# Wide matmuls in q, k and the down projections, a final norm taken in behind the transposes, and other orders in attention

## What is computed

```python
for i in range(DEPTH):                       # DEPTH = 4
    kind = i % N_MIXERS                      # 0 mLSTM, 1 windowed, 2 neighbourhood attention
    mod = (silu(cond) @ ada_w[i] + ada_b[i]).reshape(6, D_MODEL)
    h = _rmsnorm(x, norm_w[i, 0]) * (1.0 + mod[1]) + mod[0]
    x = x + mod[2] * mixer(h)
    h = _rmsnorm(x, norm_w[i, 1]) * (1.0 + mod[4]) + mod[3]
    x = x + mod[5] * _conv_ffn(h, ffn_w_up[i], ffn_conv_w[i], ffn_conv_b[i], ffn_w_down[i])
y = _rmsnorm(x, final_norm_w)
```

## Time and profile before

| | |
|---|---|
| median of 3 executions | 1898.17 us (1898.11 to 1900.09) |
| profiled execution | 1898.71 us, span of its instructions 1896.9 us |
| TensorE busy | 1835.8 us, 97% of the span |
| VectorE busy | 1312.5 us, 69% |
| ScalarE busy | 980.9 us, 52% |
| GpSimd busy | 177.7 us, 9% |
| mean granted TensorE clock | 0.990 of full |
| memory traffic | 418 MB, mean 220 GB/s |

### The profile page before, as it was taken

One profiled execution on the slowest core, in us unless ns is written; L12 is line 12 of the kernel. 1 busy time (PEld: TensorE's weight loads), 2 busy tenths in 40 slices (PEclk: granted clock), 3 DMA queues, 4 the chain that ended last, 5 costly groups with the idle time before them and its releaser, 6 DMA issues.

```text
span 1896.9 us, 29734 instructions
## 1 busy us (share of the span) xinstructions
PE 1835.8 (97%) x12336; PEld 1577.7 (83%) x12336; DVE 1312.5 (69%) x1871; ACT 980.9 (52%) x1453; POOL 177.7 (9%) x154
## 2 busy tenths in 40 slices
PE   5999999999999999999999999999999999999998
PEld 2999877797889867889976778898999777988898
DVE  2854677667896566898555688956654776669974
ACT  1754344545674454676344466745643445447752
POOL 2100121001000112000111210002100220020001
PEclk9999999999999999999999999999999999999999
DMA  8565656866554657655574766556555647645451
GB/s 350 198 225 189 203 181 246 315 232 270 236 198 179 267 221 293 241 226 184 194 296 151 291 268 259 181 195 240 226 181 170 222 174 283 256 164 191 179 194 50
DMA packets 72535, 418.26 MB, mean 220 GB/s; under 512 B 12176, under 2 KB 18696, under 8 KB 24144
## 3 DMA queue, kind: packets, MB, share of 16 engines
q1 hardware_dynamic: 53856, 392.19, 55.3%
q10 hardware_dynamic: 18544, 24.17, 4.0%
HBM read 405.35 MB, written 10.95 MB: 219 GB/s over the span
## 4 chain that ended last, share of the span: by engine, by line
PE 88%; DVE 5%; DMA 2%; ACT 2%; issue 2%; POOL 1%; ACTq 0%; POOLq 0%; SPq 0%; DVEq 0%
PE ps L560 17%; PE ps L578 9%; PE ps L562 9%; PE ps L612 6%; PE ps L614 6%; PE ps L613 6%; PE ps L543 6%; PE ps L545 6%; PE ps L544 6%; PE ps L594 4%; PE ps L625 3%; DMA raw<-in_stream 2%; DVE spl_lo L466 1%; PE ps L831 1%; PE ps L816 1%
## 5 line engine op out<-in xcount | busy, mean ns | idle before, releaser
L466 DVE TENSOR_TENSOR spl_lo<-raw,spl_hi 128x1024 fp32r<-128x1024 f32 x556 | 687.7, 1259 | 275.3 <-ACT spl_hi L455 274.3
L455 ACT ACTIVATE spl_hi<-raw 128x1024 fp32r<-128x1024 f32 x556 | 573.9, 1052 | 327.0 <-PE ps L614 161.5
L560 PE MATMUL ps<-H,spl_hi 128*128 128x512 f32 x1408 | 497.5, 399 | 3.4 <-DVE H L1669 3.4
L562 PE MATMUL ps<-H,spl_lo 128*128 128x256 f32 x1408 | 393.9, 280 | 0.0
L560 PEld LDWEIGHTS ps<-H,spl_hi 128*128 128x128 f32 x1408 | 265.0, 188 | 78.2 <-issue 14.6
L562 PEld LDWEIGHTS ps<-H,spl_lo 128*128 128x128 f32 x1408 | 266.1, 189 | 0.0
L612 PE MATMUL ps<-G_hi,spl_hi 128*128 128x256 f32 x704 | 199.2, 283 | 0.0
L613 PE MATMUL ps<-G_lo,spl_hi 128*128 128x256 f32 x704 | 199.2, 283 | 0.0
L614 PE MATMUL ps<-G_hi,spl_lo 128*128 128x256 f32 x704 | 199.2, 283 | 0.0
L543 PE MATMUL ps<-H,spl_hi 128*128 128x256 f32 x512 | 148.2, 289 | 6.8 <-DVE H L1669 5.2
L544 PE MATMUL ps<-H,spl_hi 128*128 128x256 f32 x512 | 146.0, 285 | 0.0
(11 more groups left out here) (241 smaller groups left out, 3226.6 us busy)
## 6 DMA issues: line engine op xcount, KB each, us to landing
raw<-in_stream SPq DMA_DIRECT2D x374, 1024.0 KB, 4.9
out_new_C<-c_stage ACTq DMA_DIRECT2D x16, 512.0 KB, 3.7
ada_b<-in_ada_b ACTq DMA_DIRECT2D x4, 768.0 KB, 9.2
E<-rows_out ACTq DMA_DIRECT2D x8, 256.0 KB, 4.3
Em<-rows_out ACTq DMA_DIRECT2D x8, 256.0 KB, 4.7
x<-in_x ACTq DMA_DIRECT2D x1, 1024.0 KB, 12.1
wide<-rows_out ACTq DMA_DIRECT2D x8, 128.0 KB, 5.2
cache<-in_na_cache ACTq DMA_DIRECT2D x1, 1024.0 KB, 9.0
```

The source lines that it names most:

```text
L455: act.activation(spl_hi[m % SPL][:, :], raw[r % RAW][:, h * HALF:(h + 1) * HALF], ACT.Copy).then_inc(S["hi_done"], 1)
L466: dve.tensor_tensor(spl_lo[m % SPL][:, :], raw[r % RAW][:, h * HALF:(h + 1) * HALF], spl_hi[m % SPL][:, :].bitcast(F32), ALU.subtract).the ...
L560: pe.matmul(banks[:, b * 512:(b + 1) * 512], w_hi, H[:, kk * 512:(kk + 1) * 512], start=kk == 0, stop=False, skip_group_check=True)
L562: mm = pe.matmul(banks[:, b * 512:b * 512 + TOK], w_lo, H[:, kk * 512:kk * 512 + TOK], start=False, stop=kk == KD - 1, skip_group_check=True)
```

## The change

- q and k are computed in wide form (`queries_keys`). `A_hi` and `A_lo` become the two halves of one tensor A, `B_hi` and `B_lo` of B, at the places that they had; a chunk's high and low columns stay 16 KB apart, and a wide matmul reads them as two runs of 256 columns (`A_both`, `B_both`). ACT copies the high half of each bank to Q or K and DVE adds the low half (`with_low`). The banks are ACC[0:4], two for each group of two tiles.
- The mLSTM and FFN down projections are wide for pairs 0 to 2 and narrow for pair 3 (`project_wide`). Pair p uses banks 2p and 2p+1; pair 3 uses ACC[0] once pair 0 has been added. The gated activations lie chunk by chunk, as H does. `residual` adds a wide pair in two passes of four instructions.
- The final norm: DVE's scaled x is transposed without the inverse root, three of four groups of transposes before the sum of squares; the root is a per-row factor when ACT and DVE evacuate the rows. The broadcast matmul and the four products fall away. Three of the four output transfers move from ACT's queue to SP's.
- One adaLN tile is placed between the halves of v; the first head of layer 0 and the last head of layer 3 have one less.
- ACT's row broadcasts of the second head of each mLSTM layer are issued behind two splits of v's weights, not in front.
- Layer 1: ACT's transposed queries(1) stands in front of exps(3). Layer 2: DVE's reciprocals(1) stands in front of the split.
- The state of the last head in layer 3 uses banks ACC[2:4], and TensorE waits for pair 2's addition before the normalisers of two norms.

```diff
+V_FILL = 1
-HEAD_FILL = {0: [3, 3, 3, 2], 3: [2, 2, 2, 2]}
+HEAD_FILL = {0: [2, 3, 3, 2], 3: [2, 2, 2, 1]}
+WIDE = [r for r in range(2 * DEPTH) if r % 2 or MIXER[r // 2] == "mlstm"]
...
-            order += [("ml_v", i, c, t) for c in range(2) for t in range(8)]
+            order += [("ml_v", i, 0, t) for t in range(8)]
+            fill(V_FILL)
+            order += [("ml_v", i, 1, t) for t in range(8)]
...
+    A = sb("A", 2 * KI * TOK, F32R, rA)
+    A_hi, A_lo = A[:, 0:KI * TOK], A[:, KI * TOK:2 * KI * TOK]
+    A_both = A[:, :].rearrange("p (e k t) -> p k e t", e=2, t=TOK)
...
+            sp.wait_ge(S["yrow_a"], 2)
+            sp.dma_start(io["y_prompt"][0, :, 0:512], yrow[:, 0:512]).then_inc(S["y_landed"], 16)
+            sp.wait_ge(S["yrow_d"], 2)
+            sp.dma_start(io["y_prompt"][0, :, 512:D], yrow[:, 512:D]).then_inc(S["y_landed"], 16)
+            sp.wait_ge(S["yrow_d"], 4)
+            sp.dma_start(io["y_sample"][0, :, 512:D], yrow[:, D + 512:2 * D]).then_inc(S["y_landed"], 16)
...
+            def queries_keys(n, k0, banks):
+                for h in range(2):
+                    m = 2 * n + h
+                    pe.wait_ge(S["lo_done"], m + 1)
+                    for k in range(4):
+                        kk = k0 + 4 * h + k
+                        for b in range(2):
+                            c = slice(k * 256 + b * P, k * 256 + b * P + P)
+                            w_hi, w_lo = spl_hi[m % SPL][:, c], spl_lo[m % SPL][:, c]
+                            pe.matmul(v3(banks[b][:, :], TOK), w_hi, B_both[:, kk], start=kk == 0, stop=False,
+                                      skip_group_check=True)
+                            mm = pe.matmul(banks[b][:, 0:TOK], w_lo, B_both[:, kk, 0], start=False, stop=kk == KI - 1,
+                                           skip_group_check=True)
+                    mm.then_inc(S["half_used"], 1)
...
+            def project_wide(n0, t, nk, r, rows, chunk, ready):
...
+                        if pair < 3:
+                            bank = ps[2 * pair + o]
+                            pe.matmul(v3(bank[:, :], TOK) if nk == KI else bank[:, :], w_hi, rows(k), start=k == 0, stop=False, skip_group_check=True)
+                            mm = pe.matmul(bank[:, 0:TOK], w_lo, chunk(k)[0], start=False, stop=k == nk - 1,
+                                           skip_group_check=True)
+                            continue
+                        if k == 0 and o == 0:
+                            pe.wait_ge(S["x_done"], 5 * r + 1)
...
                 if q in (1, 2 * DEPTH - 1):
+                    pe.wait_ge(S["x_done"], 5 * (q - 1) + 3)
                     normalisers()
...
-                    if t % 2 == 0:
-                        pe.wait_ge(S["qk_evac"], 8 * j + t // 2 + 1)
-                    weights_stationary(n0 + t, both(B_hi, B_lo), 8 * (t % 2), UP[(t // 2) % 2], t % 2 == 0, t % 2 == 1)
+                    if t % 2 == 0 and 4 * j + t // 2 >= 2:
+                        pe.wait_ge(S["qk_sum"], 2 * (8 * j + t // 2) - 2)
+                    queries_keys(n0 + t, 8 * (t % 2), ACC[t // 2 % 2 * 2:t // 2 % 2 * 2 + 2])
...
-                pe.wait_ge(S["qk_evac"], 2 + 8 * (j + 1))
+                pe.wait_ge(S["qk_sum"], 16 * (j + 1))
...
-                    project(n0, t, 2 * NJ, both(G_hi, G_lo), ready)
+                    project_wide(n0, t, 2 * NJ, 2 * i + 1, lambda k: G[:, k * 512:(k + 1) * 512], both_of(G), ready)
...
-            norm(2 * DEPTH)
             for g in range(4):
-                pe.wait_ge(S["hm_done"], 4 * 2 * DEPTH + g + 1)
+                if g == 3:
+                    square_sums(2 * DEPTH)
+                if g < 2:
+                    pe.wait_ge(S["x_done"], 5 * (2 * DEPTH - 1) + 3)
+                pe.wait_ge(S["xa_done"], g + 1)
                 for s in range(NS):
                     for c in range(2):
                         k = 2 * g + c
-                        mm = pe.transpose(ACC[g][:, s * TOK + c * P:s * TOK + (c + 1) * P],
-                                          yT[:, k * TOK + s * T:k * TOK + (s + 1) * T], ident)
+                        mm = pe.transpose(ROWS[g][:, s * TOK + c * P:s * TOK + (c + 1) * P],
+                                          xa[:, k * TOK + s * T:k * TOK + (s + 1) * T], ident)
...
-                    copy(K[:, g * 512:(g + 1) * 512], UP[g % 2][:, :], "qk_evac")
+                    for b in range(2):
+                        copy(K[:, g * 512 + b * TOK:g * 512 + (b + 1) * TOK], ACC[g % 2 * 2 + b][:, 0:TOK], "qk_evac")
...
-                for h in range(2):
-                    state_rows(j, h)
+                state_rows(j, 0)
...
+                        if half == 0 and t == 1:
+                            state_rows(j, 1)
...
+                    queries(1, ACC[0])
                     exps(3)
-                    queries(1, ACC[0])
...
+            act.wait_ge(S["rstd_done"], 2 * DEPTH + 1)
+            for s in range(NS):
+                for g in range(2):
+                    act.wait_ge(S["yt_mm"], g + 1)
+                    act.activation(y_columns(s, g), ROWS[g][:, s * TOK:(s + 1) * TOK], ACT.Identity,
+                                   scale=rstd[:, s:s + 1]).then_inc(S["yrow_a"], 1)
...
+                wide = WIDE.index(r) if r in WIDE else None
+                if wide is not None and pair < 3:
+                    for e in range(2):
+                        for c in range(4):
+                            k, s = divmod(4 * pair + c, NS)
+                            o = slice(k * TOK + s * T, k * TOK + (s + 1) * T)
+                            ins = dve.scalar_tensor_tensor(x[:, o], ps[k][:, e * TOK + s * T:e * TOK + (s + 1) * T],
+                                                           coef_g[r % 2][:, NS * k + s:NS * k + s + 1], x[:, o],
+                                                           ALU.mult, ALU.add)
+                        ins.then_inc(S[("x_half", "x_done")[e]], 1)
+                        if e == 0:
+                            dve.wait_ge(S["x_half"], 3 * wide + pair + 1)
...
+                def with_low(dst, g, done, scale):
+                    for b in range(2):
+                        o = slice(g * 512 + b * TOK, g * 512 + (b + 1) * TOK)
+                        dve.wait_ge(S["qk_evac"], 16 * j + 2 * done + b + 1)
+                        dve.scalar_tensor_tensor(dst[:, o], ACC[g % 2 * 2 + b][:, TOK:2 * TOK], scale, dst[:, o], ALU.mult,
+                                                 ALU.add).then_inc(S["qk_sum"], 1)
...
                     maxima(1)
+                    reciprocals(1)
                     split("qkv", i, 1, 1, 0)
-                    reciprocals(1)
```

More of the change, by code:

```diff
@@ L596, in half_rows @@
                                                stop=t == h == k == 1 and a is a_lo, skip_group_check=True)
+                    mm.then_inc(S["half_used"], 1)
+            def project_wide(n0, t, nk, r, rows, chunk, ready):
+                for h in range(2):
+                    m = 2 * (n0 + t) + h
+                    pe.wait_ge(S["lo_done"], m + 1)
+                    ready(2 * t + h)
+                    for c in range(8):
+                        pair, k, o = unit(16 * t + 8 * h + c, nk)
+                        w_hi, w_lo = (w[m % SPL][:, c * P:(c + 1) * P] for w in (spl_hi, spl_lo))
+                        if pair < 3:
[6 more added lines that the diff above has]
+                            pe.wait_ge(S["x_done"], 5 * r + 1)
+                        x_hi, x_lo = chunk(k)
+                        out = ACC[0][:, o * TOK:(o + 1) * TOK]
+                        st, en = k == 0 and o == 0, k == nk - 1 and o == 1
+                        pe.matmul(out, w_hi, x_hi, start=st, stop=False, skip_group_check=True)
+                        pe.matmul(out, w_hi, x_lo, start=False, stop=False, skip_group_check=True)
+                        mm = pe.matmul(out, w_lo, x_hi, start=False, stop=en, skip_group_check=True)
                     mm.then_inc(S["half_used"], 1)
@@ L687, in norm @@
                     if late:
-                        state(1, MH - 1, range(2, 3), ACC[0:2])
+                        state(1, MH - 1, range(2, 3))
                     fill(between)
@@ L691, in norm @@
                     if late:
-                        state(1, MH - 1, range(3, 4), ACC[0:2])
+                        state(1, MH - 1, range(3, 4))
                 fill(after)
@@ L818, in values, with state @@
                     mm.then_inc(S["half_used"], 1)
-            def state(j, h, parts=range(4), banks=ACC[2:4]):
+            def state(j, h, parts=range(4)):
                 q = 4 * j + h
@@ L1153, in norm @@
                 if late:
-                    state(1, MH - 1, range(3), ACC[0:2])
+                    state(1, MH - 1, range(3))
                 for g in range(4):
@@ L1630, in mod_columns, with scaled @@
                                                   nw.unsqueeze(2).to_broadcast([P, KD, 2]), ALU.add, ALU.mult))
-            def scaled(pair):
```

(8 more changed lines are left out.)

85 lines of the change are left out of this document (44 added, 41 removed).

## The result

The changed kernel takes 1871.74 us (median, 1869.12 to 1873.76), the kernel before, timed beside it, 1898.11 (1892.71 to 1900.09): a ratio of 0.9876, 95% interval 0.986 to 0.9893, so 26.4 us less. Timed twice more, beside experiments, it took 1873.65 against 1893.26 (ratio 0.9895, 0.988 to 0.9911) and 1873.11 against 1893.17 (0.9893, 0.9879 to 0.9908), 20 us less. The forecast, 1876 and 22 us less, lies between.

A forecast was written before the change was run, and what follows sets the result against it. TensorE, busy 1835.8 of 1896.9 us, was taken as the bound. Terms 12.3 + 1.8 + 5.0 + 0.3 + 4.5 - 1.2 = 22.7 us, off the median 1898.17, gave 1875.5, said as 1876; range 1867 to 1887.

The forecast's parts named there:

- Wide units: q, k, mixer and FFN down projections: 1232 units made wide save 0.010 us each, 12.3 us; 3.4 to 16.3.
- the middle: Pace of a wide unit taken as 0.350 us, between 0.3536 and 0.3468 seen in the FFN's up projection.
- End of k: TensorE waits for the last group's copies and dependent DVE sums: cost 0.6 us per layer, 1.2 us; 0.4 to 2.
- The tile in v: An adaLN tile of 0.9 us fits in TensorE's 1.4 us wait mid-v: gain 1.8 us over two layers; 1 to 2.
- DVE at pair ends: Wide pairs' eight DVE adds instead of four delay the next weight split 1.2 us, covered by about 1.4 us: no cost.
- 18 pair ends: Ends of wide down-projection pairs; without the cover of about 1.4 us, each would cost what is missing.
- Layer 2: Attention, reciprocal of unit 1 before DVE's split: 4.3 us of idle plus 1 us at half clock, taken as 5.0; 2 to 6.5.
- Late next: Layer 2 attention: after the reciprocal moves, the copy of the query rows, still behind the split, is what comes late.
- Layer 1: Attention, transposed q copied before unit 3's exponentials: the stall moves to GpSimd's scaled weights; gain 0.3 us, 0 to 2.
- The end: Final norm and output: scaling in the evacuation, transposes some 0.3 us late, landing at 1892.4; gain 4.5 us, 3 to 5.5.
- Rival E: Whole kernel, everything at its upper end: 30 us less, 1868 us; chance 0.10.
- The total: Whole kernel: terms sum to 22.7 us less, span 1896.9 to 1874.2; off the median 1875.5, said as 1876.

The follow-up runs named there:

- the experiment: Changed kernel with layer 2's reciprocal of unit 1 put back behind DVE's split of weights: 1877.66 us, ratio 0.9915 to the kernel before.
- the grouped kernel: Changed kernel with neighbouring units' matmuls ordered wide, wide, narrow, narrow in all wide stages, FFN up included: 1865.21 us, ratio 0.9851; repeated, 1865.89 us, 0.9866.

## Why the prediction was right, step by step

- **Wide units, 12.3 us: right.** The stages gave 12.1, and splitting the matmuls again cost 11.5. The choice of the middle, 10 ns a unit, came out because both paces occur: 0.3535 in q and k of layer 0, the first quarter of q and k of layer 3, both mixer downs and the last FFN down, 0.3467 in the rest of layer 3's q and k and in three FFN downs. That they occur in about equal parts is luck; nothing in the prediction said which stage gets which. That the two runs of A and B cost nothing was chosen without a row; layer 3's q and k at 0.3466 show it. By the Trainium skill's rule on non-contiguous patterns ("PSUM — Partial Sum Buffer", Specifications (TRN2)), read for the moving operand too, these stages would have lost; the trace shows no such loss. The Trainium skill's rule of columns / 2.4 GHz plus 2.5 ns ("TensorE: Matmul & The Clock Gate", "Wait — 56ns, not 53.3ns?") gave an estimate of 3 us for the whole, and the stages show 12.1.
- **End of k, -1.2 us: right.** The wait rose from 0.7 to 1.3 us a layer; the chain has two sums, 0.75 us, behind ACT's copies where the wait had only the copy.
- **The tile in v, 1.8 us: 1.3 to 1.4.** The mechanism holds, the size was too high. The wait fell from 1.4 to 0.4 us, but the tile takes 1.06 us there, so v's stage kept its 95.8 us and the saving is what the heads no longer hold: 0.9 in layer 0, 0.5 in layer 3, where the heads' tile probably covered some idle time (no run shows that part).
- **DVE at pair ends, nothing: right, but with a wrong count.** "18 pair ends" with a cover of 1.4 us are ten, with 1.2 to 1.4, and eight with about 4.
- **Layer 2, 5.0 us: 4.8, and 4.6 by the experiment.** Late next is what was named. The next rows start 3.8 us earlier, not 4.3 (5.2 us behind the unit's last exponential, where it was 9.0): the prediction left the split its 2.4 us, and beside GpSimd it took 2.9. The rest, 0.8 to 1.0 us, is the work that no longer runs at the clock of 0.50, as foretold.
- **Layer 1, 0.3 us: 0.7, not shown.** The wait for the transposed q (2.2 us) is gone and the waits for exponentials and scaled weights behind it rose by 2.2 together, so the stall moved as foretold. But from the layer's first product to its output projection the kernel before takes 67.1 us, and the kernels that have the changed order take 65.1 to 67.2 in their traces; 0.7 lies within that scatter. No experiment took this line alone.
- **The end, 4.5 us: 4.1 to 4.2.** From the last product to the root's end it is 3.8 us against 3.6, so the transposes cost 0.2, not 0.3. ACT's four operations follow each other every 0.39 us, not 0.50. Against that, the last transfer is home 3.2 us after its issue, not 2.3; all four are issued within 1.3 us. The misses nearly cancel.
- **Rival E, 1868: added up too low.** It takes 1 us for layer 1, whose upper end is given as 2, and 1 us of cost for the end of k, whose lower end is 0.4. With these ends the sum is 31.9 us and the rival 1866, just outside the stated range.
- **The total.** 22.7 us against 26.8 by the profiled executions, of which 4.9 are the startup, norms, up stages and an output projection of those two executions. The two later timings, near 20 us, are about as far on the other side: the kernel before had a median of 1898.1 in one set of timings and of 1893.2 to 1894.8 in three others. The forecast is as good as these measurements can say; its agreement to the microsecond in any one of them would be luck.

## What to carry to other kernels

Cost a change in the form of matmuls by the pitch of starts in a long undisturbed stretch, never by the durations of the groups, and look at several such stretches: one row of instructions can have more than one pace. When TensorE waits long for another engine, read that engine's order for a short operation that stands behind a long one; moving it costs next to nothing (here 0.6 us on the long one, which then ran beside GpSimd), and the clock comes back with it. Before the remainder of a difference is put down to the change, look whether the same kernel shows it in each of its traces. Work added beside the bound is priced by the cover at each place where the bound needs its product, counted place by place.

## What was not expected of the hardware

- A row of alternating 512- and 256-column matmuls has two stable paces, 0.3467 and 0.3535 us a unit, with periods of two and three units. A break in the row can switch them; both occur on either layout of the operands. Two long ones followed by two short ones have a single pace, 0.3483. Why is open: the trace has the starts, but not what holds each of them.
- Matmuls of 256 columns alone start every 0.120 us; between long ones they take 0.115 (0.23 for two in the grouped kernel's chain), and the long ones 0.233.
- The last transfer of 256 KB takes 2.3 us from the end of its issue to the end of the span with ACT issuing two by two, and 3.2 us with four issued within 1.3 us. That the number under way at once is the cause is likely, not shown.
- A split of a half tile on DVE (128x1024, two inputs) takes 1.22 us alone and up to 2.3 us beside an operation of GpSimd.
